# Differential attention outputs: transposed by DMA instead of by TensorE, their norm weights folded into the output projection

## What is computed

```python
def diff_attention(q, k, v, slopes, lam, lam_init, subln_g):      # 4 heads, each 2 q/k maps of 64, v of 128
    ...
        p = jax.nn.softmax(s, axis=-1)                            # causal, with ALiBi
        a = p[:, :, 0] - lam * p[:, :, 1]
        return jnp.einsum('bhqk,bkhd->bqhd', a.astype(v.dtype), v)
    ...
    o = rms_norm(o, subln_g) * (1.0 - lam_init)                   # per head, over its 128 values
    return o.reshape(B, S, H * DIFF_V_DIM)

def hybrid_mixer(...):
    ...
    return jnp.concatenate([o_d, o_l], axis=-1) @ w_out           # 512 differential and 512 dilated columns
```

## Time and profile before

| | |
|---|---|
| median of 3 runs | 2526.93 us (2526.12 to 2528.03) |
| the profiled execution | 2526.12 us, span of its slowest core 2524.6 us |
| spans of the 8 cores | 2508.7 to 2524.6 us |
| TensorE, VectorE, ScalarE, POOL busy | 97%, 73%, 56%, 16% of the span |
| attention stage, first to last transposition | 880.2 to 1630.9 us |

### The profile page before, as it was taken

One profiled execution on the slowest core, in us unless ns is written; L12 is line 12 of the kernel. 1 busy time (PEld: TensorE's weight loads), 2 busy tenths in 40 slices (PEclk: granted clock), 3 DMA queues, 4 the chain that ended last, 5 costly groups with the idle time before them and its releaser, 6 DMA issues.

```text
span 2524.6 us, 49509 instructions; the slowest of 8 cores (2508.7 to 2524.6 us)
## 1 busy us (share of the span) xinstructions
PE 2438.3 (97%) x16530; PEld 1289.9 (51%) x16530; DVE 1853.5 (73%) x3187; ACT 1426.2 (56%) x2080; POOL 408.4 (16%) x470
## 2 busy tenths in 40 slices
PE   6999999999999999999999999999999999999998
PEld 4544444444444556666555666544444444444457
DVE  6767987897887763556687545589777967967974
ACT  4534653753643576677686767765435535535433
POOL 1210310220221211101013111013102101200302
PEclk8999999999999999999999999999999999999999
DMA  6975775675588954526359554267345535535734
GB/s 122 185 150 140 189 134 141 171 148 136 160 169 173 186 151 79 79 48 159 93 132 230 95 86 64 55 176 246 94 136 150 168 122 162 176 98 158 215 126 142
DMA packets 154968, 356.15 MB, mean 141 GB/s; under 512 B 28416, under 2 KB 39296, under 8 KB 154112
## 3 DMA queue, kind: packets, MB, share of 16 engines
q1 hardware_dynamic: 129872, 260.89, 34.6%
q0 software_dynamic: 24848, 92.09, 23.9%
HBM read 381.84 MB, written 80.48 MB: 183 GB/s over the span
## 4 chain that ended last, share of the span: by engine, by line
PE 91%; DVE 3%; issue 2%; ACT 2%; DMA 1%; POOL 0%; DVEq 0%; ACTq 0%; POOLq 0%; SPq 0%
PE ps L968 42%; PE ps L1037 21%; PE ps L1173 9%; PE ps L1319 5%; PE ps L1135 4%; PE ps L1210 3%; PE ps L1277 3%; PE ps L1448 2%; ACT M L653 2%; PE ps L1411 1%; DVE M L650 1%; DMA M<-x 0%; DVE M L725 0%; DMA M<-xT 0%; PE ps L715 0%
## 5 line engine op out<-in xcount | busy, mean ns | idle before, releaser
L653 ACT ACTIVATE M<-ps 128x1024 bf16<-128x1024 f32 (+9 forms) x1179 | 879.0, 782 | 567.3 <-PE ps L1037 171.3
L968 PE MATMUL ps<-M 128*128 128x512 f16 (+1 forms) x5096 | 1077.0, 373 | 11.3 <-DVE M L650 4.8
L650 DVE TENSOR_TENSOR M<-M 128x512 bf16<-128x512 bf16 (+10 forms) x1608 | 932.0, 613 | 189.3 <-ACT M L653 87.7
L968 PEld LDWEIGHTS ps<-M 128*128 128x128 f16 x5096 | 499.6, 98 | 583.4 <-issue 17.7
L653 ACT ACTIVATE M<-M 128x512 f32<-128x512 f32 (+4 forms) x648 | 384.0, 617 | 426.8 <-DVE M L650 372.8
L1037 PE MATMUL ps<-M 128*128 128x512 f16 (+2 forms) x2926 | 540.5, 345 | 1.2 <-DVE M L650 0.6
L650 POOL TENSOR_TENSOR M<-M 128x512 f32<-128x512 f32 (+3 forms) x238 | 292.5, 1236 | 1320.7 <-DVE M L791 638.8
L1037 PEld LDWEIGHTS ps<-M 128*128 128x128 f16 x2926 | 273.6, 98 | 261.8 <-issue 1.6
L650 DVE TENSOR_TENSOR M<-ps,M 128x1024 f32<-128x1024 f32 (+5 forms) x322 | 304.4, 947 | 112.6 <-PE ps L1037 73.0
L1173 PE MATMUL ps<-M 128*128 128x512 f16 x1024 | 261.1, 381 | 10.5 <-DVE M L1120 6.1
L650 DVE TENSOR_TENSOR M<-M,ps 128x512 f16<-128x512 f32 (+1 forms) x182 | 120.7, 665 | 72.3 <-PE ps L968 43.7
(11 more groups left out here) (55 smaller groups left out, 801.9 us busy)
## 6 DMA issues: line engine op xcount, KB each, us to landing
M<-x SPq DMA_DIRECT2D x128, 512.0 KB, 6.5
M<-cgu SPq DMA_DIRECT2D x88, 512.0 KB, 4.3
M<-xT SPq DMA_DIRECT2D x64, 512.0 KB, 6.8
x<-M SPq DMA_DIRECT2D x64, 512.0 KB, 6.2
M<-wgu POOLq DMA_DIRECT2D x58, 512.0 KB, 8.0
M<-cdn SPq DMA_DIRECT2D x38, 704.0 KB, 4.3
M<-wd POOLq DMA_DIRECT2D x32, 704.0 KB, 6.7
M<-c1g SPq DMA_DIRECT2D x30, 512.0 KB, 4.7
```

The lines of the kernel that those rows point to most:

```text
L650: return lambda e: e.tensor_tensor(o, a, b, op)
L653: return lambda e: e.activation(o, i, f, **k)
L968: g.pe([(lambda e, gg=gg, kc=kc, pb=pb, src=src, piece=piece, n=n, w=w, cs=cs: e.matmul(bank(pb + gg)[:, 0:w], src[:, gg * 512 + kc * 128: ...
```

## The change

The transposition moves from TensorE to a DMA. `epilogue` now issues, as its last operation, one transposing DMA of 128x512 f16 on SP's queue from `Otok` straight into the mix tile; the identity, the bank, the four matmuls, the eviction and the list `urgent` go, and with them the due time `EPI`. The norm's weights are multiplied into the first four blocks of each `wout` tile after its load instead (rows of the output weights that belong to the differential values), one 128x512 f16 multiply in place on VectorE or ScalarE. Nothing else is changed.

```diff
@@ Sched.dma
-        for out, in_ in pairs:
+        for out, in_, *tr in pairs:
             tb.dcnt[eng] += 16
-            self.q[eng].append(lambda e, out=out, in_=in_: e.dma_start(out=out, in_=in_).then_inc(sem, 16))
+            kw = {"transpose": True} if tr else {}
+            self.q[eng].append(lambda e, out=out, in_=in_, kw=kw: e.dma_start(out=out, in_=in_, **kw).then_inc(sem, 16))
@@ late_consts
-            g.dma(POOL, [(ident[:], ident_d)], aft, [B_ident], 64)
@@ wout_w
                     g.dma(POOL, [(v, wout_d[d])], [], [b], 512)
+                    h = v[:, 0:512]
+                    g.op([(DVE, v_16(512), lambda e: e.tensor_scalar(h, h, gains[:, 48:49], None, ALU.mult)),
+                          (ACT, a_sb(512) + 0.09, act_(h, h, AF.Copy, scale=gains[:, 48:49]))], [b, B_gain], [b],
+                         port=True)
@@ fill_one
-                if urgent and not state["open"] and (urgent[0][0] <= g.clock or not fillq):
-                    urgent.popleft()[1]()
-                    return True
...
@@ epilogue
-                    nom = g.clock + EPI
-
-                    def transposes():
-                        if s > 0:
-                            need(("wout", s - 1, Q))
-                        pb = pbank()
-                        pv = bank(pb)[:, 0:256].bitcast(F16)
-                        g.pe([(lambda e, tq=tq: e.transpose(pv[:, tq * 128:(tq + 1) * 128], Otok[ti][:, tq, :], ident[:]),
-                               [B_Otok[ti], B_ident], [B_ps[pb]], tq == 3) for tq in range(4)], 4 * c_mm(128), nom=nom)
-                        g.op([(DVE, 0.45, lambda e: e.tensor_scalar(mixT[u][:, ts(Q)], pv, gains[:, 48:49], None,
-                                                                    ALU.mult)),
-                              (ACT, a_ps(512) + 0.09, act_(mixT[u][:, ts(Q)], pv, AF.Copy, scale=gains[:, 48:49]))],
-                             [B_ps[pb], B_gain], [B_mix[u][Q]], pen=EVPEN)
-                        done.add(("mix", s, u, Q))
-                    urgent.append((nom, transposes))
+                    if s > 0:
+                        need(("wout", s - 1, Q))
+                    g.dma(SP, [(mixT[u][:, ts(Q)].rearrange("p (a c) -> p a c", a=4),
+                                Otok[ti].rearrange("p a c -> p (a c)"), True)], [B_Otok[ti]], [B_mix[u][Q]], 256)
+                    done.add(("mix", s, u, Q))
```

More of the change, by code:

```diff
@@ L455, in _consts @@
     tri = (np.arange(128)[None, :] >= np.arange(128)[:, None]).astype(np.float32)
-    ident = np.eye(128, dtype=np.float32)
-    return tri, ident
+    return tri
 NL = NF // 2
@@ L462 @@
 LOOK = 5
-EPI = 9.0
 OUT7 = 3
@@ L501, in build_program @@
     dec_d = dt_in("c_dec", [128, 4])
-    ident_d = dt_in("c_ident", [128, 128])
     outT_d = nc.dram_tensor("outT", [NSEQ, D, SEQ], F32, kind="ExternalOutput").ap()
@@ L540, in build_program @@
         tri = sb("tri", [128, 128], BF16)
-        ident = sb("ident", [128, 128], F16)
         ones_bf = sb("ones_bf", [128, 128], BF16)
@@ L553, in build_program @@
         B_ps = [Buf("ps%d" % i, psum=True) for i in range(8)]
-        B_gain, B_dec, B_tri, B_ident, B_ones, B_lamv, B_lam = (
-            Buf(n) for n in ("gain", "dec", "tri", "ident", "ones", "lamv", "lam"))
+        B_gain, B_dec, B_tri, B_ones, B_lamv, B_lam = (
+            Buf(n) for n in ("gain", "dec", "tri", "ones", "lamv", "lam"))
         B_sml = [[Buf("sml%d_%d" % (i, j)) for j in range(5)] for i in range(3)]
@@ L1092, in attention @@
             fillq = deque()
-            urgent = deque()
             done = set()
@@ L1231, in fill_one @@
                 if pre is not None and not all(t in done for t in pre):
-                    if urgent and not state["open"]:
-                        urgent.popleft()[1]()
-                        return True
                     return False
@@ L1540, in attention @@
                     mdone += x[0] + x[2]
-                    while (state["f"] - f0) / fw < mdone / total[w] or (urgent and not state["open"] and urgent[0][0] <= g.clock):
+                    while (state["f"] - f0) / fw < mdone / total[w]:
                         if not fill_one():
@@ L1549, in attention @@
             fillq.extend(out_items(NSEQ - 1, NTT - 1))
-            while fillq or urgent:
+            while fillq:
                 assert fill_one()
@@ L1655, in _prep_weights @@
     out["c_lam"] = np.ascontiguousarray(np.broadcast_to(lam[None, :], (128, 256))).astype(f32)
-    tri, ident = _consts()
+    tri = _consts()
     out["c_tri"] = tri
@@ L1660, in _prep_weights @@
     out["c_strip"] = _strip()
-    out["c_ident"] = ident
     return out
```

## The result

The changed kernel takes 2500.88 us (median of 4 runs, 2498.50 to 2503.16); the kernel before, on the same chip, 2527.45 us. The ratio is 0.9896, with a 95% interval of 0.9878 to 0.9913: 26.6 us faster, where 10.2 was forecast.

The account below looks back on a forecast made before the run. TensorE, 97% busy, was taken as the bound. Removed work -11.3, folded weights +0.3 and late instructions +0.8 gave -10.2 us, so 2526.9 us became 2516.7 us, with a range of 2509 to 2532 us.

Parts of the forecast that it names:

- The removed work: Attention stage: dropping 128 transposition matmuls from TensorE saves 7.0 to 15.6 us, taken as the middle, 11.3 us.
- the filler bank: Attention stage: TensorE's 6.1 us of waits for VectorE's evictions of this bank, given no credit in the sum.
- rival D: Attention stage: matmuls' whole durations go, 2497.7 us, or their waits and filler-bank waits go, 2505.2 us; chance 0.03.
- late instructions: Attention stage: added DMA work lengthens TensorE's waits that no engine ends, 10.6 us before; cost 0.8 us.
- Busy time: Sign to look for in TensorE's attention stage: busy time lower by about 7 to 10 us.
- Evictions: Attention stage: 26 on VectorE and 6 on ScalarE go, 16.7 us of those engines; nothing credited.
- The folded weights: Output weights: 16 added multiplies, 6.7 to 10.9 us of engine time, nearly all covered; cost 0.3 us.
- The DMAs: SP's queue: 32 added, landing in 2.0 to 20.6 us; latency costs nothing below 24 us.
- The unit ends: Differential units' ends: without the transposition's turn, the next projection gets the other bank; reason for the 15.6 us upper bound.
- B: Attention stage: 7.0 us go, but waits move on and scalings are uncovered, 6.7 us; 2526.6 us, chance 0.22.
- C: Unit starts: transposing DMAs delay TensorE's instructions, 2.65 us in each of 8 differential units; 2537.9 us, chance 0.13.

Follow-up runs that it names:

- x9: Changed kernel plus four constant-tile matmuls after each epilogue, as their own piece in the accumulator bank just emptied; 0.9924 of the kernel before, 2508.2 us.
- x6: Changed kernel plus four constant-tile matmuls at the head of each of 32 dilated-unit Q projection fillers; 0.9928 of the kernel before, 2509.3 us.
- x2: Changed kernel plus the four TensorE transpositions per epilogue into a filler bank, without eviction, DMA kept; 0.9998 of the kernel before, 2526.9 us.
- x5: As x2, but the four matmuls per epilogue read a constant tile, so never wait for Otok; 0.9984 of the kernel before, 2523.4 us.
- x3: Changed kernel plus a filler-bank turn and an eviction of 256 float32 columns per epilogue, no transpositions; 0.9910 of the kernel before, 2504.7 us.
- x11: Changed kernel without the 16 multiplies of the output weights, norm's weights left out; 0.9920 of the kernel before, 2507.2 us.
- x4: Changed kernel without any transposition: no DMA, VectorE writes untransposed values straight into the mix tile; 0.9918 of the kernel before, 2506.7 us.
- x13: As x5, but each piece due at once after its epilogue, not 9 us later; 0.9945 of the kernel before, 2513.5 us.
- x7: Kernel before with the planner's noise on (seed 1), due times jittered by up to 0.4 us; 1.0039 of the kernel before, 2537.3 us.
- x8: Changed kernel with the same planner noise as x7; 0.9955 of the kernel before, 2516.1 us.

## Why the prediction was right in its sign and wrong in its size

**The removed work** is the step that failed, at its bound: "Upper: 9.9 + 5.7 = 15.6 us, if all of them go". It counts what stands on the transpositions' own line and takes that as all that their removal can give. Their time was read well: 7.0 us by starts against 7 and 8 in x9 and x6, and 7.9 in the mean of the cores once the clock is taken out. But put back as they were they cost 26 (x2), and on ready operands still 22 (x5); the wait for Otok itself is the 3.5 us between the two, not told apart from none and within my 5.7. Two terms had been put at nothing.

The first is waits on other lines. All waits fell by 12.6 us in the mean of the eight cores, where the transpositions' own are 5.7; the scores' waits for ScalarE alone fell by 7.1. I had named these (7.3 and 5.5 us) as waits of the stage and left them out of the sum; only the 6.1 us of the filler bank went into rival D, which had 0.03. Why they go when the matmuls go is open, see below.

The second is late instructions and the clock. I had late instructions as a cost of the DMAs only, +0.8 us, and not as something that the old order paid and a new one need not; in the mean of the cores they fell by 2.2 us. And I had priced waits at their length only: the clock, which I read as at its upper level nearly all the time, gives back some 4.5 us in the mean and 7.2 on the slowest cores.

**Busy time** of the whole run fell by 13.3 us, where 7 to 10 were forecast; the excess is that clock, as far as the estimate in the section on the result goes.

**Evictions** without credit: nothing speaks against it; x3 puts bank and eviction together at 3.5 us, below what can be told.

**The folded weights**: 10.9 us on ScalarE, at the upper end of 6.7 to 10.9, and covered, as said; without them (x11) nothing is gained.

**The DMAs**: landing of 4.2 us in the median, between the bounds of 2.0 and 20.6, and 21.9 at most on any core, still below the 24 us that would have mattered; no wait for them; x4 without them no faster. That each holds SP's queue, for 1.2 to 10.0 us, I had only among the signs of being wrong and without a price. Loads of x were not late for it: other engines waited 8.0 us for them in the stage, 10.0 before.

**The unit ends.** The bank's turn that I gave as a reason for the upper bound: in x3 that turn is kept and costs 3.5 us, so it is not shown to be worth anything.

**The rivals.** B, the waits move on: the opposite held, waits elsewhere fell. C: late instructions are there, and in the 6.93 us wait a transposing DMA was in flight; but such waits are fewer than before, and with the casts spread they are gone though the DMAs are still there, so it takes the bunched casts. Whether the DMAs add to them is not told: 1.9 us in the mean of the cores without the DMAs (x4), 4.5 in the changed kernel, but also 1.9 in x6, which has them. D came nearest, 2505.2 us by its second form, but by the filler bank's 6.1 us, while the projections' waits for VectorE fell by 1.6 in the mean of the cores, and not by the scores' waits, which fell most. The Trainium skill ("VectorE: DVE Perf Modes", section "The three transpose paths") makes the crossbar the slower path, 1309 ns for a 128x128 block against 390 ns on TensorE. No run here times a single block; for the kernel it did not decide, since TensorE is 97% busy and no engine's wait is put down to a transposing DMA.

**Open.** Why a piece of 0.22 us, due 9 or 20 us after the epilogue, costs 0.7 us in all. x9 and x13 suggest that an early place is cheaper, by 10 us with the bank kept; but every edit makes the planner order the whole stage anew, which alone is worth 5 to 15 us (x4, x11, x7, x8), and no run here moved the piece and kept all else in its place. How bank, place and the planner's order share the 15 us is therefore not settled, and neither is why the scores' waits fall with the change: x3 has them without the matmuls.

## What to carry to other kernels

On the engine that sets the time, the price of a small piece of work is not its length and its own wait: leave it out, or put it in again with ready operands, and time that; here 0.22 us cost 0.2 to 0.3 us in two orders of the stage and 0.6 to 0.8 in five others, and the difference stood on lines that had nothing to do with it. When an order is planned by hand or by program, time two or three jittered orders of each version before believing a difference that such a jitter can make, here up to 15 us. And where the trace shows waits that no engine ends, look for bunched transfers and spread them.

## What the hardware showed that was not expected

With two or three memory-to-memory weight casts issued in a bunch, TensorE stood for 1.1 to 6.9 us at a time (35 waits of over 1 us) in the middle of ready work, with a packet of instructions arriving at each; with the same casts spread over a unit these waits fell to 0.2 us per core in the mean, in both kernels (6.7 and 4.5 before). Such a wait can cost more than its length: behind 16 of the 35 the granted clock fell, and around the end of the 6.93 us one its mean was 0.54 over 7 us. A transposing DMA of 128x512 f16 from SBUF to SBUF holds SP's queue for 1.2 to 10.0 us (median 1.66; up to 14.2 on another core), while a plain load of x there takes 0.37 in the median.
